# A decoder layer's tail in four pieces woven into the samples' attention, and branch A's scores for four chunks at once

## The chip, the cores and the metric

The kernel runs on one core of one Trainium2 chip. The metric is the device time of one execution in microseconds, the median of several. All data is float32.

## The reference, cut to what matters

One layer serves 1024 prompt tokens and 8 samples of 4 tokens each. The samples attend over 8192 cached tokens, in 64 pages of 128 per sample.

```python
u = rmsnorm(h); qa, kv_a, qi, ki, wi, qb, kv_b, g_a, g_b = project(u @ w_in)
# branch A: top-k keys by an indexer, then softmax(q k) v over 8 heads, 2 key heads of 64
# branch B: (softmax(Q1 K1) - lam softmax(Q2 K2)) V over 4 heads of 128, rmsnorm per head
merged = sigmoid(g_a) * (o_a @ w_br_a) + sigmoid(g_b) * (o_b @ w_br_b)
h = h + rmsnorm(merged @ w_out, attn_post_g)
gate, up = split(rmsnorm(h, ffn_pre_g) @ w_gate_up)
h = h + rmsnorm((silu(gate) * up) @ w_down, ffn_post_g)
y = h + sigmoid(h @ w_ple_gate) * (p_i @ w_ple_proj)
```

The lines from `merged` on are what this document calls the tail. They need only the attention's output `o` of the same token.

## The kernel before

Five engines run their own queues: TensorE (PE) multiplies, VectorE (DVE) and ScalarE (ACT) do the elementwise work, GpSimd (POOL) and SyncE (SP) mostly issue DMAs. They wait for each other by semaphores. The program is a sequence of stages, each a block whose end all engines meet: the projections, the prompt's selection and attention, the samples' attention (`sample_attend`), and the last stage (`tail`).

**The tail of the layer** is the class `Tail`. Tokens lie along columns, features along partitions. It works through pieces of columns; per piece there are units in a fixed order: `ma` and `mb` (the two branches' projections, 8 of each, alternating), `wo` (8), the norm `n1`, the updates `a1`, `n2`, `a2`, `gg` and `up` (22 of each), `d0`, `d1`, `dn` (the down projection, 8 outputs in three parts), `n3`, `a3`, then 8 times `yg`, `yp` and the transposition `yt` with the store of y. A unit has a number `g`; `at` finds it, `done_by` says which count of the semaphore `done` it raises. Every unit of weights is one DMA from `packed` into one of four slots (`SLOTS`): 256 KB for `ma` and `mb`, 512 KB for `wo`, `gg`, `up`, `yg`. SP issues the load for the unit four further on when a unit is done (`sync`, L1379). At the last `dn` of a piece SP issues the loads of o and of the gates for the next piece (`load_inputs`, L1383, L1387), and at its last `yt` those of h and of the embedding (`load_stream`, L1391, L1392). Two PSUM banks take turns. A float32 matmul shows as two records on PE.

**Who computes which columns.** `sample_attend` holds a `Tail` named `tw` with three pieces of 304 columns, prompt tokens 0 to 911. The last stage has its own `Tail` named `tp` with one piece of 144 columns: prompt tokens 912 to 1023 and the 32 samples' tokens.

**The samples' attention** goes through 64 chunks of 8 pages, 8 chunks per sample, in the steps that the list `steps` holds. A step has the scores of the chunk before, the transposition of this chunk's keys on DVE (`keys` in two parts for branch B, L1976, and `keys_a`, L1984), and the values of a chunk ten steps back. The scores of branch B (L1798) are 64 matmuls of 32x32 weights on 256 columns on all 16 places of the PE array: row group k by head h. The scores of branch A (L1808) wait for every second chunk: for `d` in 4 and `k` in 4 and the two chunks `i`, 32 matmuls on the 8 places k by i. After the fourth chunk of a half, ACT copies branch B's scores from the PSUM bank (`b_out`, L1917), DVE adds the selection to branch A's (`a_out`, L1993), reads both for the maxima (L1997), and at a sample's end the softmax follows.

**The order** is written out by a small planner: each unit of `tw` has a cost (`cost`), and each step gets an equal share of the sum of the costs less `LEAD` (20) and `RESERVE` (60); units are put between slots of a step as their budget allows, and the rest follow after the last step. All engines go through this one order; DVE and ACT take the units a little later (`late`). At the end SP stores the samples' attention output, `out_b` and `out_a`, to `o_t` in memory (L1777, L1779), and the last stage reads it back as columns of its o. The stretch between these two blocks is called the seam below.

Of the kernel before, what the change touches and what calls it, by code (L numbers as in the profile page):

```python
# [1296 lines left out]
STARTS = [0, WOVEN, 2 * WOVEN]  # L1297


class Tail:  # L1300
# [6 lines left out]
    def __init__(self, nc, a, ctx, name, ident, ones, banks, starts, width):  # L1307
        ph = Phase(nc, ctx, name)
        self.width, self.rows, self.left, self.nb, pieces = width, width // P, width % P, len(banks), starts
# [12 lines left out]
        for g, (p, kind, n) in enumerate(self.units):  # L1322
# [3 lines left out]
            if kind[0] != "a":  # L1326
# [8 lines left out]
        self.gates = self.x[:, KC:3 * KC].rearrange("p (g n) t -> p g n t", g=2)  # L1335
        self.w = ph.sb("w", [P, self.SLOTS, 8, P])
        self.ple = ph.sb("ple", [P, 2, width])
        self.y_t = ph.sb("y_t", [P, 2, width])
        self.y_row = ph.sb("y_row", [P, 2, self.rows + 1, P])
# [9 lines left out]
         self.rooted, self.normed, self.h_set, self.sig_set, self.y_set) = (  # L1349
            ph.sem(n) for n in ("done", "o_in", "gates_in", "h_in", "ple_in", "gains_in", "z_set", "squared", "summed", "changed",  # L1350
                                "rooted", "normed", "h_set", "sig_set", "y_set"))
# [14 lines left out]
    def cost(self, g):  # L1366
        p, kind, n = self.units[g]
        scale = self.width / 352
# [12 lines left out]
    def load_inputs(self, sp, p):  # L1381
        cols = slice(self.pieces[p], self.pieces[p] + self.width)
        sp.dma_start(self.o, self.a["o_t"].rearrange("(k p) t -> p k t", p=P)[:, :, cols]).then_inc(self.o_in, 16)  # L1383
        if p == 0:
            for at in range(self.SLOTS):
                self.load_weights(sp, at)
        sp.dma_start(self.gates, self.a["gate_t"][:, :, :, cols]).then_inc(self.gates_in, 16)  # L1387

    def load_stream(self, sp, p):
        cols = slice(self.pieces[p], self.pieces[p] + self.width)  # L1390
        sp.dma_start(self.h[:], self.a["xp_t"][:, 0:KC, cols]).then_inc(self.h_in, 16)  # L1391
        sp.dma_start(self.ple[:], self.a["xp_t"][:, KC:KC + 2, cols]).then_inc(self.ple_in, 16)  # L1392
# [8 lines left out]
    def sync(self, sp, g):  # L1401
# [7 lines left out]
        if kind == "yt":  # L1409
            sp.wait_ge(self.freed_by(g), self.freed_at(g))  # L1410
            first, full, end = self.pieces[p], self.pieces[p] + self.rows * P, self.pieces[p] + self.width
            cols = slice(n * P, (n + 1) * P)
            sp.dma_start(self.a["y"][first:full, cols].rearrange("(j p) c -> p j c", p=P), self.y_row[:, n % 2, 0:self.rows, :]).then_inc(self.stored[n % 2], 16)
            sp.dma_start(self.a["y"][full:end, cols], self.y_row[0:self.left, n % 2, self.rows, :]).then_inc(self.stored[n % 2], 16)
            if n == KC - 1 and p + 1 < len(self.pieces):
                self.load_stream(sp, p + 1)
# [5 lines left out]
    def tensor(self, pe, g):  # L1422
# [3 lines left out]
        bank = self.bank(g)  # L1426
        if self.freed_at(g) > 1:
            pe.wait_ge(self.freed_by(g), self.freed_at(g) - 1)
        if kind in ("n1", "n2", "n3"):
            pe.wait_ge(self.summed, 24 * p + {"n1": KC, "n2": 2 * KC, "n3": 3 * KC}[kind])  # L1430
            pe.matmul(bank[:, 0:self.width], self.ones[:], self.sumsq[:], start=True, stop=True).then_inc(self.done, 1)  # L1431
            return
        if kind == "yt":
            pe.wait_ge(self.y_set, p * KC + n + 1)
            for j in range(self.rows + 1):
                rows = min(P, self.width - j * P)
# [13 lines left out]
        for k in range(lo, hi):  # L1450
# [7 lines left out]
            ins = pe.matmul(bank[:, 0:self.width], self.w[:, at % self.SLOTS, k - lo, :], moving[:, k, :], start=(k == 0), stop=(k == depth - 1))  # L1458
        ins.then_inc(self.done, 1)

    def scalar(self, act, g):
        nc, (p, kind, n) = self.nc, self.units[g]
        bank = self.bank(g) if g in self.bank_of else None
        if kind in ("wo", "dn"):
# [4 lines left out]
            nc.scalar.activation(self.sq[:, i % 2], bank[:, 0:self.width], ACT.Square).then_inc(self.squared, 1)  # L1469
            nc.scalar.copy((self.u if kind == "wo" else self.z)[:, n], bank[:, 0:self.width]).then_inc(self.freed_by(g), 1)  # L1470
        if kind in ("n1", "n2", "n3"):
            act.wait_ge(self.freed_by(g), self.freed_at(g))
            nc.scalar.activation(self.rstd[:], self.rstd[:], ACT.Sqrt).then_inc(self.rooted, 1)  # L1473
        if kind == "a1":
# [3 lines left out]
            nc.scalar.activation(self.sq[:, i % 2], self.h[:, n], ACT.Square).then_inc(self.squared, 1)  # L1478
        if kind == "gg":
# [4 lines left out]
            nc.scalar.activation(self.sig[:, n % 2], bank[:, 0:self.width], ACT.Sigmoid).then_inc(self.sig_set, 1)  # L1484
        if kind == "yg":
# [3 lines left out]
            nc.scalar.activation(self.sig[:, n % 2], bank[:, 0:self.width], ACT.Sigmoid).then_inc(self.freed_by(g), 1)  # L1489
        if kind == "yt":  # L1490
# [3 lines left out]
            nc.scalar.copy(self.y_row[:, n % 2, 0:self.rows, :], bank[:, 0:self.rows * P].rearrange("p (j c) -> p j c", c=P))  # L1494
            nc.scalar.copy(self.y_row[0:self.left, n % 2, self.rows, :], bank[0:self.left, self.rows * P:(self.rows + 1) * P]).then_inc(self.freed_by(g), 1)

    def add_square(self, dve, i):
        nc = self.nc
        dve.wait_ge(self.squared, i + 1)
        dve.drain()  # L1500
        if i % KC == 0:
            nc.vector.tensor_copy(self.sumsq[:], self.sq[:, i % 2]).then_inc(self.summed, 1)
        else:
            nc.vector.tensor_tensor(self.sumsq[:], self.sumsq[:], self.sq[:, i % 2], ALU.add).then_inc(self.summed, 1)  # L1504

    def vector(self, dve, g):
        nc, (p, kind, n) = self.nc, self.units[g]
        bank = self.bank(g)[:, 0:self.width] if g in self.bank_of else None
        if kind == "ma":
            if n == 0:  # L1510
                dve.wait_ge(self.gates_in, 16 * (p + 1))
            dve.wait_ge(self.done, self.done_by[g])
            nc.vector.tensor_tensor(self.z[:, n], bank, self.gates[:, 0, n], ALU.mult).then_inc(self.freed_by(g), 1)
        if kind == "mb":
            dve.wait_ge(self.done, self.done_by[g])
            nc.vector.tensor_tensor(self.sig[:, n % 2], bank, self.gates[:, 1, n], ALU.mult).then_inc(self.freed_by(g), 1)
            dve.drain()
            nc.vector.tensor_tensor(self.z[:, n], self.z[:, n], self.sig[:, n % 2], ALU.add).then_inc(self.z_set, 1)
        if kind in ("wo", "dn"):
            self.add_square(dve, self.of_square(p, kind, n))  # L1520
        if kind in ("n1", "n2", "n3"):
# [6 lines left out]
            nc.vector.tensor_scalar(self.rstd[:], bank, 1.0 / D, 1e-6, ALU.mult, ALU.add).then_inc(self.freed_by(g), 1)  # L1528
            dve.wait_ge(self.rooted, 3 * p + which + 1)
            nc.vector.reciprocal(self.rstd[:], self.rstd[:])  # L1530
            dve.drain()
        if kind in ("a1", "a2", "a3"):
            gain = self.gains[:, int(kind[1]) - 1, n:n + 1]
            if kind == "a2":
                nc.vector.scalar_tensor_tensor(out=self.z[:, n], in0=self.h[:, n], scalar=gain, in1=self.rstd[:], op0=ALU.mult, op1=ALU.mult).then_inc(self.normed, 1)  # L1535
                return
            src = (self.u if kind == "a1" else self.z)[:, n]
            dve.drain()
            nc.vector.scalar_tensor_tensor(out=self.sig[:, n % 2], in0=src, scalar=gain, in1=self.rstd[:], op0=ALU.mult, op1=ALU.mult)  # L1539
            dve.drain()  # L1540
            nc.vector.tensor_tensor(self.h[:, n], self.h[:, n], self.sig[:, n % 2], ALU.add).then_inc(self.changed if kind == "a1" else self.h_set, 1)  # L1541
# [4 lines left out]
        if kind == "gg":  # L1546
            dve.wait_ge(self.sig_set, p * self.F_TILES + n + 1)
            nc.vector.tensor_tensor(self.sig[:, n % 2], bank, self.sig[:, n % 2], ALU.mult).then_inc(self.freed_by(g), 1)  # L1548
        if kind == "up":
            dve.wait_ge(self.done, self.done_by[g])  # L1550
            dve.drain()
            nc.vector.tensor_tensor(self.act_t[:, n], bank, self.sig[:, n % 2], ALU.mult).then_inc(self.freed_by(g), 1)
        if kind == "yp":
# [3 lines left out]
            nc.vector.tensor_tensor(self.sig[:, n % 2], bank, self.sig[:, n % 2], ALU.mult).then_inc(self.freed_by(g), 1)  # L1557
# [3 lines left out]
            nc.vector.tensor_tensor(self.y_t[:, n % 2], self.h[:, n], self.sig[:, n % 2], ALU.add).then_inc(self.y_set, 1)  # L1561
# [20 lines left out]
def sample_attend(nc, a):  # L1582
# [8 lines left out]
    with ExitStack() as ctx:  # L1591
# [10 lines left out]
        key_a = ph.sb("key_a", [P, 2 * CH, 4, 32])  # L1602
# [47 lines left out]
        rest = Tail(nc, a, ctx, "tw", ident, ones, t_bank, STARTS, WOVEN)  # L1650
# [12 lines left out]
        squared, ms_ready, meaned, rooted, finished, stored = (ph.sem(n) for n in ("squared", "ms", "meaned", "rooted", "finished", "stored"))  # L1663
# [31 lines left out]
        costs = [rest.cost(u) for u in range(len(rest.units))]  # L1695
# [13 lines left out]
        order += [("rest", u) for u in range(g, len(costs))]  # L1709
# [30 lines left out]
        def _(sp):  # L1740
# [44 lines left out]
        def _(pe):  # L1785
            def scores(c):
# [183 lines left out]
        def _(dve):  # L1970
# [8 lines left out]
            def turn_keys_a(c):  # L1979
                dve.wait_ge(ka_in[c % 2], (c // 2 + 1) * CH * 16)  # L1980
                if c % 2 == 0 and c:
                    dve.wait_ge(a_scored, c // 2)
                at = c % 2 * CH
                nc.vector.transpose(key_a[:, at:at + CH].rearrange("p g n s -> p (g n s)"),  # L1984
# [14 lines left out]
            def set_q(b):  # L1999
                if b:  # L2000
                    dve.wait_ge(a_scored, 4 * b)
# [219 lines left out]
```

## Time and profile before

| | us |
|---|---|
| median of 3 runs | 3236.38 (3230.28 to 3241.0) |
| profiled execution, its own time | 3238.8 |
| span of its trace | 3237.3 |
| PE busy | 2876.3 (89%) |
| DVE busy | 1461.4 (45%) |
| POOL, ACT busy | 678.3, 588.2 |
| records on PE | 26593 |

Busy is the time in which an engine had an instruction in work; matmuls overlap each other in the pipeline, so their mean duration is longer than the distance of their starts. The granted clock (PEclk) is given in tenths of the full TensorE clock over 40 equal slices of 80.9 us. In the views, `tw_` names are buffers of the woven tail, `tp_` those of the last stage, `sa_` those of the samples' attention; L numbers are lines of the kernel before.

### The profile page before, as it was taken

What the parts mean: (1) busy time and instruction counts of PE and PEld (TensorE: products, weight loads), DVE (VectorE), ACT (ScalarE), POOL (GpSimd) and SP (SyncE); (2) the same over time, 40 slices, a digit from 0 to 9 for tenths busy, and PEclk for the clock granted to TensorE, in tenths of its full rate; (3) what the DMA queues carried; (4) which work ended last, traced back from release to release, by engine and by line L of the source; (5) the groups of instructions that cost most, each with busy time, mean ns of one, the idle gap of its engine ahead of it and who ended that gap; (6) DMA issues with size and microseconds to landing.
All of it is one profiled execution on the core that took longest, in us unless ns stands there. A gap on an engine that the chain in (4) does not pass through costs nothing. (4 is left out here: it accounts for less than half of the span.)

```text
span 3237.3 us, 69341 instructions
## 1 busy us (share of the span) xinstructions
PE 2876.3 (89%) x26593; PEld 2020.4 (62%) x26593; DVE 1461.4 (45%) x3004; ACT 588.2 (18%) x1308; POOL 678.3 (21%) x1192
## 2 busy tenths in 40 slices
PE   8998979998789669999978889999798799998698
PEld 4764534665466446666755567766566576675698
DVE  2337858996788354333343443323433632002211
ACT  2431112001566110101011110010100201001101
POOL 0131003001100001133332433333333333430000
PEclk9999989999899889999998999999899899999799
DMA  7575239422500757789888988888888896662586
GB/s 226 148 226 181 79 117 305 128 79 87 164 8 18 223 182 245 241 299 315 297 303 271 310 297 276 308 305 302 300 282 276 268 300 235 223 204 91 174 266 197
DMA packets 419892, 708.73 MB, mean 219 GB/s; under 512 B 67985, under 2 KB 230193, under 8 KB 419442
## 3 DMA queue, kind: packets, MB, share of 16 engines
q1 hardware_dynamic: 330674, 470.65, 44.5%
q0 software_dynamic: 75456, 232.86, 21.7%
q8 instruction: 211, 3.46, 0.4%
q10 hardware_dynamic: 13440, 0.85, 0.3%
q14 instruction: 111, 0.91, 0.1%
HBM read 660.01 MB, written 92.13 MB: 232 GB/s over the span
## 5 line engine op out<-in xcount | busy, mean ns | idle before, releaser
L1458 PE MATMUL sa_t<-tw_z,tw_w 128*128 128x304 f32 x2496 | 679.8, 428 | 14.8 <-DVE tw_z L1535 10.7
L1458 PEld LDWEIGHTS sa_t<-tw_z,tw_w 128*128 128x128 f32 x2496 | 470.5, 192 | 195.3 <-issue 44.4
L1736 POOL DMA_DIRECT2D sa_ring_v<-cache_b_kv x512 | 275.2, 537 | 1211.5 <-PE sa_o L1865 850.4
L1458 PE MATMUL sa_t<-tw_x,tw_w 128*128 128x304 f32 x1440 | 406.0, 438 | 43.4 <-DMA tw_w<-packed 37.8
L1976 DVE STREAM_TRANSPOSE sa_key_b<-sa_ring_k 128x2048 f32<-128x2048 f32 x128 | 294.9, 2307 | 263.9 <-PE sa_s L1798 194.1
L1458 PEld LDWEIGHTS sa_t<-tw_x,tw_w 128*128 128x128 f32 x1440 | 277.5, 197 | 151.5 <-issue 64.6
L414 PE MATMUL pr_acc<-pr_w,pr_u_t 128*128 128x512 f32 (+1 forms) x720 | 288.1, 548 | 3.8 <-DVE pr_row L574 3.7
L1737 POOL DMA_DIRECT2D sa_ring_va<-cache_a_kv x512 | 274.2, 536 | 54.1 <-issue 27.0
L874 PE MATMUL sel_g<-sel_u,sel_gw 128*128 128x352 f32 x768 | 227.5, 459 | 0.0
L1798 PE MATMUL sa_s<-sa_key_b,sa_q_pad 32*32 32x256 f32 x8192 | 191.9, 416 | 26.1 <-DVE sa_key_b L1976 19.3
L874 PEld LDWEIGHTS sel_g<-sel_u,sel_gw 128*128 128x128 f32 x768 | 145.8, 190 | 81.9 <-issue 0.8
L414 PEld LDWEIGHTS pr_acc<-pr_w,pr_u_t 128*128 128x128 f32 x720 | 125.3, 198 | 112.8 <-issue 108.3
L1798 PEld LDWEIGHTS sa_s<-sa_key_b,sa_q_pad 32*32 32x32 f32 x8192 | 123.7, 107 | 82.1 <-issue 32.1
L1861 PE MATMUL sa_o<-sa_ring_v,sa_prob_t 128*8 128x128 f32 x4096 | 142.5, 280 | 26.3 <-DMA sa_ring_va<-cache_a_kv 19.9
L1861 PEld LDWEIGHTS sa_o<-sa_ring_v,sa_prob_t 128*8 128x8 f32 x4096 | 102.1, 91 | 78.3 <-issue 54.6
L1484 ACT ACTIVATE tw_sig<-sa_t 128x304 f32<-128x304 f32 x66 | 28.0, 424 | 542.7 <-PE sa_t L1458 542.7
L1458 PE MATMUL sa_t<-tw_h,tw_w 128*128 128x304 f32 x384 | 113.3, 450 | 12.8 <-DVE tw_h L1541 5.6
L1548 DVE TENSOR_TENSOR tw_sig<-sa_t,tw_sig 128x304 f32<-128x304 f32 x66 | 30.9, 468 | 190.3 <-ACT tw_sig L1484 190.0
L1458 PE MATMUL ta_bank<-tp_z,tp_w 128*128 128x144 f32 x832 | 105.3, 291 | 3.6 <-DVE tp_z L1535 2.4
L1458 PEld LDWEIGHTS ta_bank<-tp_z,tp_w 128*128 128x128 f32 x832 | 104.8, 194 | 4.3 <-issue 4.3
L1504 DVE TENSOR_TENSOR tw_sumsq<-tw_sumsq,tw_sq 128x304 f32<-128x304 f32 x63 | 30.0, 476 | 171.2 <-ACT tw_sq L1469 166.2
L1469 ACT ACTIVATE tw_sq<-sa_t 128x304 f32<-128x304 f32 x48 | 20.3, 423 | 463.3 <-PE sa_t L1458 463.3
(336 smaller groups left out, 3499.7 us busy)
## 6 DMA issues: line engine op xcount, KB each, us to landing
sa_ring_k<-cache_b_kv SPq DMA_DIRECT2D x512, 256.0 KB, 4.0
sa_ring_v<-cache_b_kv POOLq DMA_DIRECT2D x512, 256.0 KB, 6.3
tw_w<-packed SPq DMA_DIRECT2D x228, 512.0 KB, 6.5
tp_w<-packed SPq DMA_DIRECT2D x76, 512.0 KB, 4.3
sa_ring_ka<-cache_a_kv SPq DMA_DIRECT2D x512, 64.0 KB
sa_ring_va<-cache_a_kv POOLq DMA_DIRECT2D x512, 64.0 KB, 6.2
packed<-w_gate_up POOLq DMA_DIRECT2D x44, 512.0 KB, 13.7
tw_w<-packed SPq DMA_DIRECT2D x48, 256.0 KB, 7.5
```

What stands on the lines that cost most here:

```text
L414: ins = pe.matmul(acc[m % ACC][:, 0:hi - lo], u_t[:, p % 2, k, :], w[:, k, lo:hi], start=(k == 0), stop=(k == KC - 1))
L874: ins = pe.matmul(g_bank[n % 4][:, 0:PIECE], gw[j % GATE_W][:, k, :], u[:, k, c * PIECE:(c + 1) * PIECE], start=(k == 0), stop=(k == KC - 1))
L1458: ins = pe.matmul(bank[:, 0:self.width], self.w[:, at % self.SLOTS, k - lo, :], moving[:, k, :], start=(k == 0), stop=(k == depth - 1))
L1469: nc.scalar.activation(self.sq[:, i % 2], bank[:, 0:self.width], ACT.Square).then_inc(self.squared, 1)
L1484: nc.scalar.activation(self.sig[:, n % 2], bank[:, 0:self.width], ACT.Sigmoid).then_inc(self.sig_set, 1)
L1504: nc.vector.tensor_tensor(self.sumsq[:], self.sumsq[:], self.sq[:, i % 2], ALU.add).then_inc(self.summed, 1)
L1548: nc.vector.tensor_tensor(self.sig[:, n % 2], bank, self.sig[:, n % 2], ALU.mult).then_inc(self.freed_by(g), 1)
L1736: pool.dma_start(ring_v[:, n % RING, :], rows_of(cache_b, page, 1)).then_inc(v_in[n // 4 % 2], 16)
L1737: pool.dma_start(ring_va[:, n % RING, :], rows_of(cache_a, page, 1)).then_inc(va_in[n // 4 % 2], 16)
L1798: ins = pe.matmul(s_bank[32 * h:32 * h + 32, k, 0:CH * 32], q_pad[rows, d, h, 24 - 8 * j:56 - 8 * j], key_b[rows, :, 4 * h + d, :], start= ...
L1861: pe.matmul(o_bank[32 * h:32 * h + 8, 0:P], prob_t[:, g, 0, at:at + 8], ring_v[:, g, h * P:(h + 1) * P], start=False, stop=False, tile_pos ...
L1976: nc.vector.transpose(key_b[:, at:at + 4].rearrange("p g n s -> p (g n s)"), ring_k[:, at:at + 4, :].rearrange("p g e -> p (g e)")).then_i ...
```

## The change

The `Tail` takes pieces as pairs of columns, each with its own width, and `sample_attend` gets a fourth, 912 to 1056. The stage `tail` is empty. The planner's costs count three pieces as before; the fourth follows after everything. The samples' part of o isn't stored and read back: a new slot `join`, after the last `a3` of the third piece, copies `out_b` and `out_a` into the columns of o on DVE. The load of the gates is two DMAs, one for each gate. `key_a` holds four chunks, and branch A's scores are computed at each fourth chunk, on 16 places.

```diff
-STARTS = [0, WOVEN, 2 * WOVEN]
+PIECES = [(0, WOVEN), (WOVEN, 2 * WOVEN), (2 * WOVEN, 3 * WOVEN), (3 * WOVEN, TOK)]
...
     def load_inputs(self, sp, p):
-        cols = slice(self.pieces[p], self.pieces[p] + self.width)
-        sp.dma_start(self.o, self.a["o_t"].rearrange("(k p) t -> p k t", p=P)[:, :, cols]).then_inc(self.o_in, 16)
+        cols, w = slice(*self.pieces[p]), self.widths[p]
+        prompt = slice(cols.start, min(cols.stop, SEQ))
+        sp.dma_start(self.o[:, :, 0:prompt.stop - prompt.start], self.a["o_t"].rearrange("(k p) t -> p k t", p=P)[:, :, prompt]).then_inc(self.o_in, 16)
         if p == 0:
             for at in range(self.SLOTS):
                 self.load_weights(sp, at)
-        sp.dma_start(self.gates, self.a["gate_t"][:, :, :, cols]).then_inc(self.gates_in, 16)
+        for g in range(2):
+            sp.dma_start(self.gates[:, g, :, 0:w], self.a["gate_t"][:, g, :, cols]).then_inc(self.gates_in, 16)
...
         if kind == "ma" and n == 0:
             pe.wait_ge(self.o_in, 16 * (p + 1))
+            if self.pieces[p][1] > SEQ:
+                pe.wait_ge(self.joined, 1)
...
+    def join_samples(self, dve, out_a, out_b):
+        nc, cols = self.nc, slice(self.sample_lo, self.sample_lo + NB * NQ)
+        last = len(self.pieces) - 2
+        dve.wait_ge(self.done, self.done_by[self.at[last, "dn", KC - 1]])
+        dve.drain()
+        nc.vector.tensor_copy(self.o[:, 4:8, cols], out_b[:])
+        for g in range(HKV):
+            for half in range(2):
+                src = out_a[g * DH:(g + 1) * DH].rearrange("p (g r e) t -> p g r e t", g=HKV, e=2)[:, g, :, half]
+                ins = nc.vector.tensor_copy(self.o[half * DH:(half + 1) * DH, 2 * g:2 * g + 2, cols], src)
+        ins.then_inc(self.joined, 1)
...
-        key_a = ph.sb("key_a", [P, 2 * CH, 4, 32])
+        key_a = ph.sb("key_a", [P, 4 * CH, 4, 32])
...
-        costs = [rest.cost(u) for u in range(len(rest.units))]
+        alone = rest.at[len(PIECES) - 1, "ma", 0]
+        costs = [rest.cost(u) for u in range(alone)]
...
-        order += [("rest", u) for u in range(g, len(costs))]
+        for u in range(g, len(rest.units)):
+            order += [("rest", u)]
+            if u == rest.at[len(PIECES) - 2, "a3", KC - 1]:
+                order += [("join",)]
...
-            sp.wait_ge(finished, 1)
-            sp.dma_start(a["o_t"][512:1024, SEQ:TOK].rearrange("(h e) t -> e h t", e=P), out_b[:]).then_inc(stored, 16)
-            for g in range(HKV):
-                sp.dma_start(a["o_t"][g * 256:(g + 1) * 256, SEQ:TOK].rearrange("(r d) t -> d r t", d=DH),
-                             out_a[g * DH:(g + 1) * DH, g * 4:(g + 1) * 4, :]).then_inc(stored, 16)
-            sp.wait_ge(stored, 48)
             rest.sync_end(sp)
...
                 ins.then_inc(scored, 1)
-                if j % 2 == 0:
+                if j < 3:
                     return
                 pe.wait_ge(turned_a, c + 1)
                 for d in range(4):
                     for k in range(4):
                         rows = slice(32 * k, 32 * k + 32)
-                        for i in (j - 1, j):
-                            ins = pe.matmul(s_bank[32 * i:32 * i + 32, k, CH * 32:2 * CH * 32], q_a[rows, d, :], key_a[rows, i % 2 * CH:(i % 2 + 1) * CH, d, :],
+                        for i in range(4):
+                            ins = pe.matmul(s_bank[32 * i:32 * i + 32, k, CH * 32:2 * CH * 32], q_a[rows, d, :], key_a[rows, i * CH:(i + 1) * CH, d, :],
                                             start=False, stop=(d == 3), tile_position=(32 * k, 32 * i), skip_group_check=True)
...
-                act.wait_ge(a_scored, 2 * n + 2)
+                act.wait_ge(a_scored, n + 1)
...
-                if c % 2 == 0 and c:
-                    dve.wait_ge(a_scored, c // 2)
+                if c % 4 == 0 and c:
+                    dve.wait_ge(a_scored, c // 4)
```

The other edits give every slice of a buffer its piece's width, and `tail` becomes `del nc, a`.

## Rows read from the trace of the kernel before

**Rows 1.** The page: span, busy share and count, granted clock in 40 slices.
```profile
span 3237.3 us, 69341 instructions
...
PE 2876.3 (89%) x26593; PEld 2020.4 (62%) x26593; DVE 1461.4 (45%) x3004; ACT 588.2 (18%) x1308; POOL 678.3 (21%) x1192
...
PEclk9999989999899889999998999999899899999799
```

**Rows 2.** Windows, samples' stage: start:end, length, busy by engine, clock, DMA share, GB/s.
```profile
1150.00:2705.00 1555.00, 1390.56 (x18419) 991.42 (x18418) 617.89 (x756) 190.44 (x370) 472.14 (x880) 0.95 0.85 285
2705.00:2990.30 285.30, 265.20 (x1759) 190.62 (x1758) 40.99 (x90) 32.65 (x71) 77.24 (x144) 0.97 0.54 177
```

**Rows 3.** PE's waits from 1150 to 2705: us in total, times, longest.
```profile
PE sa_t L1458 <- DMA tw_w<-packed: 24.8, 10, 7.4
PE sa_t L1431 <- DVE tw_sumsq L1504: 22.3, 6, 7.4
PE sa_s L1798 <- DVE sa_key_b L1976: 19.3, 3, 11.3
...
PE sa_o L1861 <- DMA sa_ring_va<-cache_a_kv: 12.4, 4, 5.0
```

**Rows 4.** Timeline of the seam: start, duration, engine, line, count, idle time before.
```profile
2989.75 0.52 PE L1437 MATMUL sa_t<-sa_ident,tw_y_t 128*128 128x128 f32 x3 [0.97 <-DVE tw_y_t L1561]
...
2996.55 0.37 SPq L1383 DMA_DIRECT2D tp_x<-o_t  x1
...
3002.09 4.18 PE L1458 MATMUL ta_bank<-tp_x,tp_w 128*128 128x144 f32 x16 [11.82 <-DMA tp_w<-packed]
...
3008.73 0.31 DVE L1513 TENSOR_TENSOR tp_z<-ta_bank,tp_x 128x144 f32<-128x144 f32 x1 [11.91 <-DMA tp_x<-gate_t]
3009.09 8.12 PE L1458 MATMUL ta_bank<-tp_x,tp_w 128*128 128x144 f32 x48 [2.83 <-DVE tp_z L1513]
...
3020.51 11.45 PE L1458 MATMUL ta_bank<-tp_x,tp_w 128*128 128x144 f32 x64 [3.30 <-DMA tp_w<-packed]
...
3033.13 15.92 PE L1458 MATMUL ta_bank<-tp_z,tp_w 128*128 128x144 f32 x128 [1.17 <-DMA tp_w<-packed]
```

**Rows 5.** Windows of the last stage.
```profile
3002.00:3033.00 31.00, 23.69 (x128) 22.54 (x128) 7.30 (x24) 0.00 (x0) 0.00 (x0) 0.77 0.71 210
3033.00:3050.00 17.00, 16.00 (x129) 15.84 (x129) 2.40 (x8) 4.12 (x17) 0.00 (x0) 1.00 0.88 276
3088.00:3198.00 110.00, 109.91 (x897) 109.81 (x896) 12.86 (x42) 8.15 (x31) 0.00 (x0) 1.00 0.84 265
```

**Rows 6.** DMA issues of the last stage: count, size, median us to landing.
```profile
tp_w<-packed SPq DMA_DIRECT2D x16, 256.0 KB, 4.6
```

**Rows 7.** Timeline around the third piece's last update, and a small DVE copy.
```profile
2091.59 0.17 DVE L2008 COPY sa_q_a<-sa_q_raw_a 128x32 f32<-128x32 f32 x1
...
2944.89 0.47 DVE L1541 TENSOR_TENSOR tw_h<-tw_h,tw_sig 128x304 f32<-128x304 f32 x1
...
2947.32 0.47 DVE L1557 TENSOR_TENSOR tw_sig<-sa_t,tw_sig 128x304 f32<-128x304 f32 x1 [1.96 <-PE sa_t L1458]
```

**Rows 8.** Groups of score matmuls: count, busy us, mean ns, idle before.
```profile
L1798 PE MATMUL sa_s<-sa_key_b,sa_q_pad 32*32 32x256 f32 x8192 | 191.9, 416 | 26.1 <-DVE sa_key_b L1976 19.3 <-issue 6.8
L1808 PE MATMUL sa_s<-sa_key_a,sa_q_a 32*32 32x256 f32 x2048 | 81.2, 383 | 11.4 <-issue 11.2
```

**Rows 9.** Timeline of PE: branch B's scores alone, then with branch A's behind.
```profile
1456.59 2.76 PE L1798 MATMUL sa_s<-sa_key_b,sa_q_pad 32*32 32x256 f32 x128
1459.28 8.45 PE L1458 MATMUL sa_t<-tw_z,tw_w 128*128 128x304 f32 x32
...
1478.66 2.56 PE L1798 MATMUL sa_s<-sa_key_b,sa_q_pad 32*32 32x256 f32 x116
...
1483.14 0.24 PE L1815 MATMUL sa_stat<-sa_k_new,sa_q_new 128*32 128x4 f32 x8
```

**Rows 10.** Timeline of DVE at the end of a half.
```profile
1995.02 1.23 DVE L1993 TENSOR_TENSOR sa_raw<-sa_s,sa_sel 128x1024 f32<-128x1024 f32 x1 [0.45 <-ACT sa_raw L1917]
```

More of the change, by code:

```diff
@@ L1305, with __init__ @@
     F_TILES = D_FF // P
-    def __init__(self, nc, a, ctx, name, ident, ones, banks, starts, width):
+    def __init__(self, nc, a, ctx, name, ident, ones, banks, pieces):
         ph = Phase(nc, ctx, name)
-        self.width, self.rows, self.left, self.nb, pieces = width, width // P, width % P, len(banks), starts
+        width, self.nb = max(hi - lo for lo, hi in pieces), len(banks)
+        self.widths = [hi - lo for lo, hi in pieces]
         self.nc, self.a, self.ident, self.ones, self.banks, self.pieces = nc, a, ident, ones, banks, pieces
@@ L1367, in cost @@
         p, kind, n = self.units[g]
-        scale = self.width / 352
+        scale = self.widths[p] / 352
         if kind in self.KINDS:
@@ L1410, in sync @@
             sp.wait_ge(self.freed_by(g), self.freed_at(g))
[L1411 to L1414, printed above, removed]
+            first, end = self.pieces[p]
+            rows, left = self.widths[p] // P, self.widths[p] % P
+            full, cols = first + rows * P, slice(n * P, (n + 1) * P)
+            sp.dma_start(self.a["y"][first:full, cols].rearrange("(j p) c -> p j c", p=P), self.y_row[:, n % 2, 0:rows, :]).then_inc(self.stored[n % 2], 16)
+            sp.dma_start(self.a["y"][full:end, cols], self.y_row[0:left, n % 2, rows, :]).then_inc(self.stored[n % 2], 16)
             if n == KC - 1 and p + 1 < len(self.pieces):
@@ L1425, in tensor @@
             return
-        bank = self.bank(g)
+        bank, w = self.bank(g), self.widths[p]
         if self.freed_at(g) > 1:
@@ L1430, in tensor @@
             pe.wait_ge(self.summed, 24 * p + {"n1": KC, "n2": 2 * KC, "n3": 3 * KC}[kind])
-            pe.matmul(bank[:, 0:self.width], self.ones[:], self.sumsq[:], start=True, stop=True).then_inc(self.done, 1)
+            pe.matmul(bank[:, 0:w], self.ones[:], self.sumsq[:, 0:w], start=True, stop=True).then_inc(self.done, 1)
             return
@@ L1434, in tensor @@
             pe.wait_ge(self.y_set, p * KC + n + 1)
-            for j in range(self.rows + 1):
-                rows = min(P, self.width - j * P)
+            for j in range(w // P + 1):
+                rows = min(P, w - j * P)
                 ins = pe.transpose(bank[0:rows, j * P:(j + 1) * P], self.y_t[:, n % 2, j * P:j * P + rows], self.ident[:])
@@ L1462, in scalar @@
         nc, (p, kind, n) = self.nc, self.units[g]
-        bank = self.bank(g) if g in self.bank_of else None
+        bank, w = self.bank(g) if g in self.bank_of else None, self.widths[p]
         if kind in ("wo", "dn"):
@@ L1493, in scalar @@
                 act.wait_ge(self.stored[n % 2], 32 * (p * KC // 2 + n // 2))
-            nc.scalar.copy(self.y_row[:, n % 2, 0:self.rows, :], bank[:, 0:self.rows * P].rearrange("p (j c) -> p j c", c=P))
-            nc.scalar.copy(self.y_row[0:self.left, n % 2, self.rows, :], bank[0:self.left, self.rows * P:(self.rows + 1) * P]).then_inc(self.freed_by(g), 1)
+            rows, left = w // P, w % P
+            nc.scalar.copy(self.y_row[:, n % 2, 0:rows, :], bank[:, 0:rows * P].rearrange("p (j c) -> p j c", c=P))
+            nc.scalar.copy(self.y_row[0:left, n % 2, rows, :], bank[0:left, rows * P:(rows + 1) * P]).then_inc(self.freed_by(g), 1)
     def add_square(self, dve, i):
-        nc = self.nc
+        nc, w = self.nc, self.widths[i // 24]
         dve.wait_ge(self.squared, i + 1)
@@ L2117, in _ @@
                     dve.drain()
-                    nc.vector.scalar_tensor_tensor(out=flat, in0=flat, scalar=gain[:, 0:1], in1=rms[:, 0], op0=ALU.mult, op1=ALU.mult).then_inc(finished, 1)
+                    nc.vector.scalar_tensor_tensor(out=flat, in0=flat, scalar=gain[:, 0:1], in1=rms[:, 0], op0=ALU.mult, op1=ALU.mult)
+                elif slot[0] == "join":
+                    rest.join_samples(dve, out_a, out_b)
 def tail(nc, a):
-    with ExitStack() as ctx:
-        ph = Phase(nc, ctx, "ta")
-        ones = ph.sb("ones", [P, P])
-        ident = ph.sb("ident", [P, P])
-        banks = [ph.ps(f"bank{c}", [P, 512]) for c in range(2)]
-        id_clear, ident_ready, ones_ready = ph.sem("id_clear"), ph.sem("ident"), ph.sem("ones")
-        rest = Tail(nc, a, ctx, "tp", ident, ones, banks, [len(STARTS) * WOVEN], TOK - len(STARTS) * WOVEN)
-        block = ctx.enter_context(nc.Block())
-        @block.gpsimd
-        def _(pool):
-            identity_on(nc, pool, ident, id_clear, ident_ready)
-        @block.sync
-        def _(sp):
-            rest.sync_begin(sp)
-            for g in range(len(rest.units)):
-                if g == 4:
-                    rest.load_stream(sp, 0)
-                rest.sync(sp, g)
-            rest.sync_end(sp)
-        @block.tensor
-        def _(pe):
-            pe.wait_ge(ident_ready, 1)
-            pe.wait_ge(ones_ready, 1)
-            for g in range(len(rest.units)):
-                rest.tensor(pe, g)
-        @block.scalar
-        def _(act):
-            rest.scalar_begin(act)
-            for g in range(len(rest.units)):
-                rest.scalar(act, g)
-        @block.vector
-        def _(dve):
-            nc.vector.memset(ones[:], 1.0).then_inc(ones_ready, 1)
-            for g in range(len(rest.units)):
-                rest.vector(dve, g)
+    del nc, a
 _WEIGHTS = ("w_in", "w_br_a", "w_br_b", "w_out", "w_gate_up", "w_down", "w_ple_gate", "w_ple_proj",
```

70 lines of the change are left out of this document (36 added, 34 removed).

## Prediction

> **What bounds the kernel now.** I read the page first: the span, the busy shares and the granted clock [rows 1]. TensorE (PE) is busy 89% of the span, and no other engine comes near. Then the windows by stage [rows 2]. From 1150 to 2705 us, where the samples' scores are made while three prompt pieces of the layer's tail are woven in, PE is busy 1390.6 of 1555 us and the DMA engines carry 285 GB/s at a share of 0.85. So PE sets the pace there, with DMA close behind. From 2705 to 2990 PE is busy 265 of 285 us. The waits of PE in the first stretch [rows 3] say what most of the other 164 us are: weights of the tail 24.8 us, the norms' sums 22.3, transposed keys 19.3, values of branch A 12.4, smaller ones below. No single wait carries the stretch; a saving of PE time there is worth most of itself, except next to a wait on DMA.
>
> The second thing the reader should see is the seam before the last stage [rows 4]. The last PE work of the samples' block ends at 2989.75 + 0.52 = 2990.3. The first load of the last stage is issued at 2996.55, PE starts at 3002.09 (11.82 us idle, on weights), idles 2.83 us more because VectorE (DVE) waits for the gates until 3008.73, then 3.30 us on weights. The `wo` units begin at 3033.13. So 42.8 us pass for the 16 `ma`/`mb` units, 128 PE records. The windows show what they cost without the seam [rows 5]: 31 us at a granted clock of 0.77 for those 128 records, against 897 records in 109.9 us at clock 1.00 later in the same stage, 0.1227 us each. The 128 would be 15.7 us of PE.
>
> **Part 1, the last stage as fourth piece.** Its units, widths (144 columns) and weight loads are those of the stage before; `wo` and all that follows cost what they did, and I leave them alone. What changes lies between 2990.3 and the first `wo`. Gone are the three stores of the samples' rows and the wait for them, the end of one block and the start of another, the first loads with nothing before them. The four weight slots are full at the seam, because the loads for `ma` 0 to `mb` 1 go out as the last `yg`/`yp` units of piece 3 finish. The loads of o's prompt rows and of the gates go out at piece 3's last `dn` unit, ahead of its third norm and all its `yg` and `yp` units. `ma` 0 can start at 2990.3.
>
> Then the loads must keep up. A unit of `ma` or `mb` is 8 records, 0.98 us. Its 256 KB load is issued when the unit four before it is done and lands 4.6 us later (median, [rows 6]). Four units therefore take 0.98 + 4.6 + about 0.1 for the issue = 5.7 us instead of 3.9. The first four wait for nothing, so the last four start at 3 x 5.7 = 17.1 and all are done at 21.0 us. Now SP's queue: it has the last y stores of piece 3, then h and the embedding (8 and 2 blocks of 128 x 144 x 4 bytes, 576 and 144 KB, two issues of about 0.5 us each) ahead of `ma` 2's weights, and their bytes share the engines: 720 KB at 210 to 276 GB/s [rows 5] is about 3 us. 24 us in all. The saving is 42.8 - 24 = 19 us. Its upper end is no wait at all: 42.8 - 15.7 = 27. Its lower end is that these units take as long as before, 3002.09 to 3033.13 = 31.0 us: 11.8, say 12. I take 19, by the landing row, which is the nearest.
>
> **The join.** Five small DVE copies replace the stores and the read back. DVE's copies of 32 columns took 0.17 us [rows 7]; the one of 128 columns lies between that and the 0.47 us of an operation on 304. Together about 1 us. They stand after the last `a3` update (2944.89 + 0.47) and before the `yp` product at 2947.32, ahead of which DVE idled 1.96 us [rows 7]. So they cost nothing; were that cover gone, the `yp` product, PE's second bank and so `yg` 1 would be late by 1 us once. Its wait on the last `dn` is met before the norm that stands ahead of it. Range 0 to 1 us. The gates as two loads instead of one per piece add one issue of SP of about 0.5 us, three times ahead of loads that PE isn't waiting for at that moment: 0 to 2 us, taken as 0. The woven order before the join doesn't move, since the budget still counts three pieces.
>
> **Part 2, scores of branch A for four chunks at once.** The same 2048 PE records remain [rows 8]; only how many run beside each other changes, 8 places of the array before, 16 after. The timeline prices it [rows 9]: scores of branch B alone, 128 records on 16 places, take 1456.59 to 1459.28 = 2.69 us. The same with a pair of chunks of branch A behind it takes 1478.66 to 1483.14 = 4.48 us. A pair, 64 records on 8 places, so costs 1.79 us. Four chunks now are 128 records on 16 places with the same shape as branch B's row, so 2.69. Per four chunks 2 x 1.79 - 2.69 = 0.89 us, times 16 = 14.2 us of PE.
>
> What of it reaches the end? Of PE's waits in that stretch 37 us are on DMA [rows 3], at places where a faster PE only waits longer, and the DMA share is already 0.85. I take three quarters, 11 us. Added is a wait: ScalarE's copy of the scores now waits for the four-chunk group, which ends 0.89 us later than the pair did. Behind it are DVE's addition of the selection (which idled 0.45 us for it at 1995.02, [rows 10]), the maxima, and behind those the transposed keys for the next chunk. PE reads these one step later, about 1555/64 = 24 us, so it is covered; without cover it costs up to 0.89 us at each of the 8 ends of a sample, 7 us. The end range is 14 down to -7.
>
> Here a rule speaks for a larger number. The Trainium skill, "TensorEngine Tiling (Array Packing)", section Theoretical Speedup, lets 32x32 tiles run independently, up to 16 times. By it four chunks would cost what two do, 1.79 us, and the part would bring 28.6 us. The trace disagrees for branch B's 16 places: 2.69 us for 8 records per place, 1.5 times the pair's 1.79 for also 8 records per place.
>
> **Sum.** 19 + 11 = 30 us. Against the profiled execution (3238.8, of which the span is 3237.3 and 1.5 lie around it): 3208.8. The median of the runs is 2.4 us lower, so 3206.
>
> **Rivals.**
> - The fourth piece starts at 2990.3, but waits on weights lower the clock as they did from 3002 to 3033 (0.77), and its first 16 units take 31 us. For it: with 5.7 us per four units PE is busy only 69% there. Against it: that clock followed 12 us of a PE at rest, and now there is none. 12 + 11 = 23: 3213. Chance 0.20.
> - The scores' gain is lost since DMA paces the stretch. For it: the share of 0.85 with windows of waits on weights and values. Against it: all PE waits on DMA are 2.4% of the stretch. 19 + 0: 3217. Chance 0.12.
> - The fourth piece never waits for weights, and all of the PE time counts: 27 + 14 = 41: 3195. For it: later in the stage the same four slots keep PE at full rate [rows 5]. Against it: a unit of 256 KB is only 0.98 us of PE. Chance 0.13.
> - Sixteen places cost no more than eight (1.79 us per group): 19 + 28.6 = 48: 3189. Against it is branch B's row. Chance 0.07.
> - Slower: the four-chunk group holds ScalarE's copy, DVE stops at its addition with the next key transposition queued behind, and PE stops at the next scores. Place: `b_out`, `a_out`, `turn_keys`, at 16 half ends. Before, PE waited for these keys 3 times, 19.3 us, the longest 11.3 [rows 3], so the two others 4.0 each. If all 16 cost 4.0 it loses 64 us against 30: 3270; it decides from 30/16 = 1.9 us each. Against it: the copy is only 0.89 us late, and a step is 24 us. Chance 0.02.
> - Both parts at their lower ends (12 - 7 = 5): 3231, no change that can be told. Chance 0.03.
>
> **How the numbers follow.** The forecast keeps 0.43, with its own range of 3200 to 3212. Within 0.3% (10 us) a measurement of this kernel can't tell a change. All cases but the last two lie over that: faster 0.95, same 0.03, slower 0.02. The range takes in the cases of 12 + 0 (3224) above, and below most of the way to the sixteen places' case: 3192 to 3224.
>
> **What would show it.** PE's rows at the seam: no idle over 2 us between the last transpose of piece 3 and `ma` 0; first `ma` to first `wo` in 20 to 28 us, with waits on `tw_w` about 5 us in sum. A four-chunk group of branch A: 128 records in about 2.7 us. DVE idle before the first `yp` product falls from 1.96 to about 1. Wrong: a first `wo` later than 31 us after the seam, groups of 3.5 us or more, or new waits of PE on key transposes. The stretch to the last scores shorter by less than 5 us would refute the three quarters.

## The result and the profile after

The change makes the kernel slightly slower: 3250.95 us (median of 7, 3242.29 to 3257.73) against 3236.38 (7, 3216.41 to 3241.48). The ratio is 1.0047, 95% interval 1.0027 to 1.0067. Forecast were 3206 us and a gain of 30. The profiled execution took 3257.73 us.

The page of the changed kernel, the lines that answer to [rows 1], and the count of instruction packets, which was 211 before as well:

```profile
span 3256.1 us, 69289 instructions
...
PE 2874.4 (88%) x26593; PEld 2011.4 (62%) x26593; DVE 1462.0 (45%) x3008; ACT 588.1 (18%) x1308; POOL 677.6 (21%) x1190
...
PEclk9999989998899889999999899999889899999899
...
q8 instruction: 211, 3.46, 0.4%
```

PE has the same 26593 records and is busy 2 us less; the span is 18.8 us longer. So PE idles more. The windows say where, beside [rows 2] and [rows 5]; the first ends with the last scores, the third is from the seam to the first `wo`, the fourth is `wo`:

```profile
1150.00:2739.40 1589.40, 1395.15 (x18414) 985.04 (x18414) 617.65 (x755) 190.31 (x370) 472.03 (x880) 0.93 0.83 279
2739.40:3024.60 285.20, 264.60 (x1764) 190.79 (x1763) 41.88 (x95) 32.79 (x72) 77.24 (x144) 0.98 0.57 186
3024.60:3049.50 24.90, 18.56 (x129) 17.42 (x128) 7.39 (x24) 0.53 (x2) 0.00 (x0) 0.93 0.69 216
3049.50:3067.00 17.50, 17.47 (x128) 17.40 (x128) 2.09 (x7) 3.22 (x14) 0.00 (x0) 0.90 0.75 248
```

The stretch with the scores grew from 1555.0 to 1589.4 us, the one behind it stayed at 285, and seam to `wo` shrank from 42.8 to 24.9. So the first part came as forecast (18 us for 19) and the second cost 34 us where 11 of gain were put.

The seam in the timeline of PE, answering to [rows 4]:

```profile
3024.10 0.52 PE L1442 MATMUL sa_t<-sa_ident,tw_y_t 128*128 128x128 f32 x3 [0.97 <-DVE tw_y_t L1570]
3024.45 4.09 PE L1465 MATMUL sa_t<-tw_x,tw_w 128*128 128x144 f32 x32
3031.53 9.34 PE L1465 MATMUL sa_t<-tw_x,tw_w 128*128 128x144 f32 x56 [2.98 <-DMA tw_w<-packed]
3042.47 4.16 PE L1465 MATMUL sa_t<-tw_x,tw_w 128*128 128x144 f32 x32 [1.61 <-DMA tw_w<-packed]
3046.83 1.22 PE L1465 MATMUL sa_t<-tw_x,tw_w 128*128 128x144 f32 x8 [0.20 <-DMA tw_w<-packed]
3049.53 17.59 PE L1465 MATMUL sa_t<-tw_z,tw_w 128*128 128x144 f32 x128 [1.48 <-DMA tw_w<-packed]
```

`ma` 0 starts without a pause, and the first four units run on full slots (32 records in 4.09 us). The first load behind them is 2.98 us late; the forecast had 1.8 us there for the landing and 3 for SP's queue. In sum PE waits 6.3 us (2.98 + 1.61 + 0.20 + 1.48) where the forecast had 8.3, and is busy 18.6 us where it had 15.7, at a granted clock of 0.93.

The join, on DVE, beside [rows 7]:

```profile
2979.80 0.23 DVE L1577 COPY tw_x<-sa_out_b 128x128 f32<-128x128 f32 x1
2979.94 0.79 DVE L1581 COPY tw_x<-sa_out_a 64x64 f32<-64x64 f32 x4
...
2981.67 0.47 DVE L1566 TENSOR_TENSOR tw_sig<-sa_t,tw_sig 128x304 f32<-128x304 f32 x1 [0.94 <-PE sa_t L1465]
```

One us in all, in a gap of DVE that shrank from 1.96 to 0.94. It cost nothing.

Now the waits of PE in the first stretch, beside [rows 3]:

```profile
PE sa_s L1827 <- issue: 34.2, 11, 3.8
PE sa_t L1465 <- DMA tw_w<-packed: 26.9, 9, 6.8
PE sa_o L1880 <- DMA sa_ring_va<-cache_a_kv: 22.3, 8, 5.3
PE sa_t L1436 <- DVE tw_sumsq L1512: 16.9, 6, 6.1
PE sa_s L1817 <- DVE sa_key_b L1995: 16.6, 3, 8.4
```

A new row leads. L1827 is branch A's group, and "issue" means that nothing which the profile shows as a releaser was missing. In the kernel before the same row stood in sixth place, in the same stretch:

```profile
PE sa_s L1808 <- issue: 11.2, 6, 3.3
```

[rows 8] show these 11.2 us too, as part of 11.4 us of idle time; the prediction doesn't ask what they are.

One group in the timeline of PE (the lines left out hold one or two records each where the groups overlap, and the last 12 of branch B):

```profile
2090.23 4.36 PE L1465 MATMUL sa_t<-tw_z,tw_w 128*128 128x304 f32 x16
2094.52 2.54 PE L1817 MATMUL sa_s<-sa_key_b,sa_q_pad 32*32 32x256 f32 x115
...
2096.92 1.45 PE L1827 MATMUL sa_s<-sa_key_a,sa_q_a 32*32 32x256 f32 x41
2101.76 3.35 PE L1827 MATMUL sa_s<-sa_key_a,sa_q_a 32*32 32x256 f32 x84 [3.39 <-issue]
```

PE stops in the middle of the group, after 44 of its 128 records. No semaphore stands there: the group's only wait is ahead of its first matmul. What happens on the DMA side, in the window from 2099 to 2100 us:

```profile
q1 hardware_dynamic: 53, 0.21, 54.3%
q0 software_dynamic: 51, 0.16, 41.5%
q8 instruction: 1, 0.02, 6.8%
```

A packet of instructions is under way, with the data queues full around it. q8 carries PE's instructions, as the counts say: its queue shows 54183 entries in the trace (matmul records, weight loads and what the sequencer does), and 211 packets make that 257 to a packet of 16 KB. Two groups of 128 records back to back are 512 entries with their weight loads and want two packets within 5.4 us; a unit of the tail, 16 records in 4.3 us, wants one in 34.

The places of the stalls bear this out. Count PE's entries in order of their start. When PE goes on after each of the 12 stalls at L1827, the entries already started are 193 or 194 more than a multiple of 256, and the number of packets started by then is that same multiple: at 1285.42 us it is 50 x 256 + 193 entries and 50 packets. The last of these packets started 2.2 to 2.8 us before PE went on and itself took about 1 us. So PE stops at the end of a packet's instructions and goes on after the next packet has come. The same holds, without an exception, for all 79 breaks of over 0.3 us inside a run of score matmuls in the traces of ten kernels (before, changed, e1 to e8). What makes the next packet start so late is not shown.

### The profile page after: what moved, and what is told of

Read it like the earlier page. It is cut to its first block, busy times and chain, and to the rows that moved or that the text cites. A ratio compares the mean times of both kernels' runs of the same rounds, so it can differ in the third digit from the quotient of the medians.

```text
span 3256.1 us, 69289 instructions
## 1 busy us (share of the span) xinstructions
PE 2874.4 (88%) x26593; PEld 2011.4 (62%) x26593; DVE 1462.0 (45%) x3008; ACT 588.1 (18%) x1308; POOL 677.6 (21%) x1190
## 3 DMA queue, kind: packets, MB, share of 16 engines
q8 instruction: 211, 3.46, 0.4%
## 4 chain that ended last, share of the span: by engine, by line
PE 48%; DMA 5%; DVE 4%; issue 4%; SPq 3%; ACT 1%; DVEq 1%; POOLq 0%; POOL 0%; ACTq 0%
PE sa_t L1465 36%; PE sa_s L1817 4%; PE sa_o L1880 3%; DMA tw_w<-packed 3%; PE sa_s L1827 2%; DMA sa_ring_k<-cache_b_kv 1%; DMA sa_ring_va<-cache_a_kv 1%; SPq L1773 1%; PE sa_stat L1857 1%; SPq L1774 1%; DVE tw_sig L1548 1%; DVE sa_key_b L1995 1%; PE sa_o L1884 1%; ACT sa_prob_t L1956 1%; DVE tw_h L1550 1%
## 5 line engine op out<-in xcount | busy, mean ns | idle before, releaser
L1465 PE MATMUL sa_t<-tw_z,tw_w 128*128 128x304 f32 (+1 forms) x3328 | 787.7, 395 | 24.0 <-DVE tw_z L1544 13.6
L1465 PEld LDWEIGHTS sa_t<-tw_z,tw_w 128*128 128x128 f32 x3328 | 577.7, 194 | 206.2 <-issue 51.9
L1465 PE MATMUL sa_t<-tw_x,tw_w 128*128 128x304 f32 (+1 forms) x1920 | 471.5, 404 | 49.7 <-DMA tw_w<-packed 44.6
L1465 PEld LDWEIGHTS sa_t<-tw_x,tw_w 128*128 128x128 f32 x1920 | 341.6, 198 | 160.1 <-issue 75.1
L1465 PE MATMUL sa_t<-tw_h,tw_w 128*128 128x304 f32 (+1 forms) x512 | 136.9, 419 | 19.1 <-DVE tw_h L1550 10.4
L1491 ACT ACTIVATE tw_sig<-sa_t 128x304 f32<-128x304 f32 (+1 forms) x88 | 34.4, 390 | 618.4 <-PE sa_t L1465 618.4
L1512 DVE TENSOR_TENSOR tw_sumsq<-tw_sumsq,tw_sq 128x304 f32<-128x304 f32 (+1 forms) x84 | 36.4, 433 | 228.0 <-ACT tw_sq L1476 222.4
L1557 DVE TENSOR_TENSOR tw_sig<-sa_t,tw_sig 128x304 f32<-128x304 f32 (+1 forms) x88 | 37.6, 428 | 223.8 <-ACT tw_sig L1491 223.6
L1465 PEld LDWEIGHTS sa_t<-tw_h,tw_w 128*128 128x128 f32 x512 | 93.8, 206 | 58.2 <-issue 19.5
L1561 DVE TENSOR_TENSOR tw_x<-sa_t,tw_sig 128x304 f32<-128x304 f32 (+1 forms) x88 | 38.1, 433 | 168.8 <-PE sa_t L1465 166.1
## 6 DMA issues: line engine op xcount, KB each, us to landing
packed<-w_gate_up POOLq DMA_DIRECT2D x44, 512.0 KB, 14.2
```

The source lines that it names most:

```text
L1465: ins = pe.matmul(bank[:, 0:w], self.w[:, at % self.SLOTS, k - lo, :], moving[:, k, 0:w], start=(k == 0), stop=(k == depth - 1))
L1512: nc.vector.tensor_tensor(self.sumsq[:, 0:w], self.sumsq[:, 0:w], self.sq[:, i % 2, 0:w], ALU.add).then_inc(self.summed, 1)
L1557: nc.vector.tensor_tensor(sig[:, n % 2], bank, sig[:, n % 2], ALU.mult).then_inc(self.freed_by(g), 1)
L1561: nc.vector.tensor_tensor(self.act_t[:, n, 0:w], bank, sig[:, n % 2], ALU.mult).then_inc(self.freed_by(g), 1)
```

## The experiments

Each kernel was timed beside the kernel before; all ratios are to it. The medians of the kernel before in the three sets of experiments were 3232.5 (e1 to e4), 3233.0 (e5 to e7) and 3232.4 (e8 and e3 again). The last column is read from the whole trace; the rows of waits above end before the last of the changed kernel's stalls and have 34.2 of its 36.4 us. e5 and e6 leave out work of the layer.

| kernel | median us | ratio (95%) | idle "issue" at branch A's scores, us |
|---|---|---|---|
| changed | 3250.95 | 1.0047 (1.0027 to 1.0067) | 36.4 |
| e1 seam only | 3216.57 | 0.9949 (0.9930 to 0.9967) | 11.3 |
| e2 four chunks only | 3265.25 | 1.0108 (1.0074 to 1.0143) | 34.9 |
| e3 group apart | 3200.29 | 0.9904 (0.9871 to 0.9937) | 0.4 |
| e4 group in halves | 3249.60 | 1.0051 (1.0032 to 1.0071) | 0 |
| e5 fewer bytes | 3178.47 | 0.9836 (0.9809 to 0.9863) | 24.6 |
| e6 half as much ahead | 3190.92 | 0.9866 (0.9839 to 0.9893) | 11.9 |
| e7 pairs apart | 3217.26 | 0.9959 (0.9944 to 0.9974) | 2.8 |
| e8 maxima later | 3205.13 | 0.9926 (0.9901 to 0.9952) | 0.4 |
| e3 again | 3198.62 | 0.9897 (0.9877 to 0.9918) | 0.4 |

**e1, seam only.** Branch A in pairs again:

```diff
-                if j < 3:
+                if j % 2 == 0:
...
-                        for i in range(4):
-                            ins = pe.matmul(..., key_a[rows, i * CH:(i + 1) * CH, d, :],
+                        for i in (j - 1, j):
+                            ins = pe.matmul(..., key_a[rows, i % 2 * CH:(i % 2 + 1) * CH, d, :],
```

> The changed kernel with branch A's scores in pairs of chunks again (8 places, key_a of two chunks); the merged fourth piece and the join stay. Theory S (the seam gave its 18 us, and the four-chunk scores took them back and more): about 3218 us, ratio to the kernel before 0.9945; piece 3 ends near 2990 us as before, first ma to first wo about 25 us; PE's idle 'issue' time before branch A's scores back to about 11 us from 36. Rival M (the merged order itself delays the samples' stretch): the end of piece 3 stays near 3020 us and the ratio at 1.00 or above.

3216.57 us, 0.9949: the seam alone gives 16 us. The last transpose of piece 3 ends at 2973.0 and the first `wo` starts at 2997.27, 24.2 us later. Theory S holds, rival M falls.

**e2, four chunks only.** The same lines the other way, in the kernel before.

> The kernel before with only branch A's scores for four chunks at once; the last stage stays a stage of its own. Theory S: the scores alone cost what the samples' stretch grew by, 34 us in the profile, so about 3236 + 25 to 35 = 3266 us, ratio 1.008 to 1.011, with some 34 us of PE idle on 'issue' before branch A's scores. Rival M: ratio at 0.996 to 1.000, as the forecast of this part had it.

3265.25 us, 1.0108. The two parts add up: -0.0051 + 0.0108 = +0.0057, within the interval of the whole. So the four-chunk scores cost some 33 to 35 us on their own, and the stalls are there without the merged piece: 34.9 us.

**e3, group apart.** The order gets a slot of its own for branch A's group, with at least 4 us of tail units ahead:

```diff
+            step += [("scores_a", s - 1)] if 0 < s <= CHUNKS and s % 4 == 0 else []
...
+                between = 0.0
+                while slot[0] == "scores_a" and between < 4.0 and g < len(costs):
+                    order.append(("rest", g))
+                    spent += costs[g]
+                    between += costs[g]
+                    g += 1
                 order.append(slot)
```

> The changed kernel, but branch A's four-chunk group no longer stands right behind branch B's scores: at least one unit of the tail (4 us of PE, few instructions) is put between. Theory I (PE runs out of instructions: 512 of them in 5.4 us, and the next 16 KB block of instructions lands too late): the idle 'issue' time before branch A's scores falls from 36 to under 10 us, the group takes 2.7 to 2.8 us, and the time falls by 25 to 35 us to 3215 to 3225, ratio 0.991 to 0.997. Rival P (sixteen places at once collide in PSUM or on their operands, or the copy behind them is late): the stall within the group stays at 3 us each and the ratio at 1.00 or more.

3200.29 us, better than the expected 3215 to 3225, and 3198.62 when run again: 16 to 18 us under e1 and about 1% under the kernel before. Its stretch up to the last scores is 53 us shorter than the changed kernel's. 33 of them are idle time of PE (161.3 for 194.2 us), and 20 are busy time, at a granted clock of 0.95 for 0.93. The same place in its timeline:

```profile
2072.30 2.76 PE L1824 MATMUL sa_s<-sa_key_b,sa_q_pad 32*32 32x256 f32 x128
2074.99 4.36 PE L1465 MATMUL sa_t<-tw_z,tw_w 128*128 128x304 f32 x16
2079.28 2.76 PE L1834 MATMUL sa_s<-sa_key_a,sa_q_a 32*32 32x256 f32 x128
2081.97 0.25 PE L1841 MATMUL sa_stat<-sa_k_new,sa_q_new 128*32 128x4 f32 x8
```

The group takes 2079.28 to 2081.97 = 2.69 us, to the hundredth what branch B's row had promised, and is not interrupted. The work in it is the same; only what stands ahead of it has changed. Rival P, a collision of sixteen places, falls. Stalls on "issue" are left elsewhere, 6.7 us before the values (L1887) among them.

**e4, group in halves.** As e3, with `d` 0 and 1 in one slot and `d` 2 and 3 in a second, tail units between.

> As the kernel with the group apart, but the group itself is cut in two halves (d 0 and 1, d 2 and 3) with another unit of the tail between. Theory I: no stalls on 'issue' in either half, the same as the kernel with the group apart or up to 10 us faster. Rival P: each half of 64 records stalls or is slower than 1.35 us; ratio at 1.00 or more.

3249.60 us, a miss: no stall in branch A's halves (7.5 us are left before branch B's scores, in 3 places), and yet 50 us slower than e3. Its waits in the same stretch:

```profile
PE sa_stat L1848 <- DVE sa_top L2055: 39.8, 7, 9.2
PE sa_t L1465 <- DMA tw_w<-packed: 29.1, 6, 11.9
PE sa_s L1824 <- DVE sa_key_b L2005: 28.0, 7, 11.2
```

This is akin to the slower rival of the prediction, in another kernel: the scores end two tail units after branch B's, and at a sample's end PE waits for DVE's maxima, 39.8 us in this window, where it was 0.5 in the changed kernel. The rival's own link, the transposed keys, has 28.0 us for 16.5 in e3. One tail unit of lateness already cost something (in e3 the wait on the maxima is 14.3 us), two cost more than they gave. The waits aren't all of the 50 us: the stretch is 58 us longer than e3's, 34 of them idle and 25 busy, at a granted clock of 0.93 for 0.95.

**e5, fewer bytes.** `pool.dma_start(ring_v[:, n % RING, 0:P], rows_of(cache_b, page, 1)[:, 0:P])`, the ring cleared once.

> The changed kernel, but of each page of branch B's values only a quarter is loaded (128 of 512 columns, the rest of the ring is set to zero once), 101 MB less in the samples' stretch. Leaves out three heads' values. Theory I with the load as cause (the block of instructions lands late because the DMA engines are full): the idle 'issue' time before branch A's scores falls below 15 us from 36. Theory I with the rate as cause (PE drinks 512 instructions faster than blocks can follow, loaded or not): it stays at 25 to 40 us. In both the time falls since values no longer wait: by 10 to 60 us.

The stalls stay at 24.6 us in 12 places, near the 25 of the rate's side and far from 15.

```profile
PE sa_s L1830 <- issue: 24.6, 12, 3.8
```

With 101 MB less they are a third shorter, so a fuller DMA lengthens them. It isn't shown to be their cause, since as many places stall as before. But the DMA share was still 0.72 here for 0.83 (1150 to 2700 us), so what an idle DMA would leave of them is open.

**e6, half as much ahead.** `for d in range(2 if j == 3 else 4)` in branch B's scores.

> The changed kernel, but branch B's scores just ahead of the four-chunk group do only half of their matmuls (d 0 and 1 of 4), in each fourth chunk. Leaves out half of that chunk's branch B scores. The two groups still stand back to back on 16 places, with 384 instructions in place of 512. Theory I: the idle 'issue' time before branch A's scores falls from 36 to what the pair had with 384 instructions, 8 to 16 us; beside the 16 x 1.35 = 22 us of PE left out the time falls by 25 us more, to about 3200. Rival P (two groups on 16 places back to back collide): 30 to 40 us of stall stay, and only the 22 us go.

```profile
PE sa_s L1827 <- issue: 11.9, 5, 4.0
```

11.9 us in 5 places, with one more stall of 3.5 us right behind a group, and 3190.92 us: 60 us for 22 us of matmuls left out. The stretch is 59 us shorter: 26 us of idle time (168.4 for 194.2), 24 of work left out, and 9 since less of the busy time lay at the lower clock. Both groups still stand back to back on the sixteen places; only their count fell, and with it the stalls. So it is the count of instructions back to back that decides, not the sixteen places.

**e7, pairs apart.** The slot of e3 for each pair of e1.

> The seam-only kernel (branch A in pairs of chunks on 8 places) with the same gap put between branch B's scores and each pair. Theory I: the 11 us of 'issue' before the pairs go too, a pair takes 1.75 us, and the time falls from 3217 by 10 to 25 us to 3192 to 3207. The kernel with the four-chunk group apart then gains only 14 us from its 16 places, or less, since it pays for 16 gaps and this for 32. Rival (the gap itself buys what it buys by the order around it, whatever the instructions): no change from 3217, within 5 us.

Here the rival holds. The pairs' stalls went from 11.3 to 2.8 us, but the time stayed (3217.26 against 3216.57). The wait for the maxima, 0.3 us in e1, took their place:

```profile
PE sa_stat L1848 <- DVE sa_top L2055: 14.7, 4, 6.0
...
PE sa_s L1835 <- issue: 2.8, 1, 2.8
```

e3 pays the same wait and is still 17 us faster, 20 by the ratio of its second run. So 16 places do bring a gain once instructions keep up, and my 14.2 us fit it. The sizes aren't separated further: the two ratios' intervals together allow 6 to 29 us (12 to 28 with the second run), and e7 has 32 gaps where e3 has 16.

**e8, maxima later.** In e3, `("top_rows", b)` stands behind the values' second part.

> The kernel with the four-chunk group apart, with one more move: at a sample's end the transposition of the maxima (top_rows) comes after the second part of the values instead of before it. There PE waited 14.3 us on DVE's maxima (4 times, longest 6.0), since the gap makes them later. Theory: PE works on values and tail units meanwhile, this wait falls below 4 us, and the time falls by 5 to 12 us to about 3188 to 3195, ratio 0.987 to 0.989. Rival: the wait only moves to the next link of the sample's end (the shifts or the exponentials behind it), and the time stays within 4 us of 3200.

3205.13 against 3198.62 for e3 beside it: not faster, and slower if anything (the two intervals overlap). Most of the wait moved a link on, as the rival said, though the time came out 5 us over the rival's 3200:

```profile
PE sa_stat L1853 <- DVE sa_top_rows L2063: 20.6, 6, 9.2
...
PE sa_stat L1847 <- DVE sa_top L2054: 8.0, 3, 4.2
```

> The same kernel as the one with the four-chunk group apart, run beside the one with the later maxima, for a comparison on one chip. Expected again at a ratio of 0.990 to the kernel before.

The version that beats both kernels is e3.

## Why the prediction was wrong

**What bounds the kernel: right.** PE paces the stretch, and a change of its time there reaches the end. Whether that is in full or three quarters, as I had counted, stays open: e3 against e7 gives 17 to 20 us, with intervals that hold 14.2, and 11 in the first run.

**The seam: right in mechanism, and in size with some luck.** 24.9 us for a forecast of 24, 17.9 saved for 19; e1 timed 16. Two errors within it cancelled: PE waited 2 us less for weights than forecast (6.3 for 8.3), and its work took 2.9 us more (18.6 for 15.7), 1.7 of them since the clock was 0.93 and not the 1.00 of the rows that I had priced it by. (The 0.1227 us per record comes out with 896 records, not 897; it changes nothing.) The `wo` units took 17.6 us for 15.9 at a granted clock of 0.90, which I had left alone; that is the small rest. The rival with 31 us at a clock of 0.77 did not come, but its direction did.

**The join, the gates, the order of units: right**, all at nothing as far as can be told: e1's 16 us leave no room for a cost that shows.

**The scores: the step that failed.** I priced four chunks at 2.69 us by branch B's row, and the price was right for a group that stands alone. What I left out is that in this kernel the group stands right behind branch B's, and that two such groups use up instructions faster than they arrive: 12 of the 16 groups were cut by a stall, 36.4 us in all, and e2 timed the part at 33 to 35 us lost where 11 were to be gained. The term was not mis-sized; a cost was missing from it, put at nothing without a reason. The account of the stretch, 34.4 us longer:

- PE's work, counted as if always at full clock, fell by 15.8 us (1316.8 for 1332.6), for a forecast of 14.2.
- Idle time of PE 194.2 for 164.4 us, +29.8. Of it "issue" at branch A's scores +23.0 (34.2 for 11.2) and the wait on branch A's values +9.9 (22.3 for 12.4); the rest comes to -3.1.
- The clock: the granted clock of the stretch fell from 0.95 to 0.93. The trace's record of the clock has PE busy for 157 us at the lower of its two levels (1.2 GHz), 116 before; 41 us more at half speed cost 20 us. That is why PE was busy for 1395.2 us, 4.6 more than before, with less work.

The sum is 29.8 + 20.4 - 15.8 = 34.4 us. So the kernel lost more than the stalls' own length. That the clock fell because of the stalls isn't shown, and the instruction stalls alone don't carry it: e4 has none in branch A's groups and 151 us of busy time at the lower level, e6 has about as many as the kernel before and 138 us. In these kernels it goes with the idle time of PE as a whole. The three kernels with 190 to 195 us idle in this stretch (changed, e2, e4) have 151 to 159 us at the lower level, those with 150 to 165 us idle have 96 to 118, and e6 with 168 lies between. No run held one of the two and moved the other.

The Trainium skill, "Runtime: NRT & Kernel Launch", section Instruction fetch mechanics, says that instructions come in 16 KiB blocks and that the cost of crossing a block's end is mostly hidden. The blocks agree (211 packets, 3.46 MB); "hidden" does not hold for groups of 21 ns per record, where a crossing showed as 2.2 to 3.9 us of idle PE in 11 of the 16 groups, and as 0.6 us in one.

**The added wait: half right.** ScalarE's copy came later, and it cost nothing noticeable in the changed kernel (0.5 us for the maxima both times). But the cover was thinner than the 24 us of a step that I gave: in e3 one tail unit of lateness (4 us) brought 14.3 us of waiting for the maxima, in e4 two brought 39.8.

**The slower rival** had the right sign and the wrong mechanism, at a chance of 0.02. The hint was in the profile: 11.2 us of "issue" in 6 stalls on L1808, up to 3.3 us each, exactly at groups of 128 and 64 records back to back. A change that puts 256 back to back had to be priced from that row: if each of the 16 groups lost 3.3 us, 53 us less 14, slower.

## What to carry to other kernels

Idle time on "issue" within a run of short PE instructions is a resource like any other; count the records per us that an edit puts back to back, and price it from the stalls already there. Packing small matmuls densely paid here only with something slow, a large matmul unit, between the dense groups. And a gap that cures one wait spends the slack of the chain behind it: one unit cost less than it gave, two cost more.

## What the hardware showed beyond that

A packet of PE's instructions is short (about 1 us), yet PE went on only 2.2 to 2.8 us after it had started, with 101 MB less to load as well as without (e5: 2.3 to 2.7 us). What differs between the stalls is how early the packet starts: in the changed kernel 10 of the 12 packets at its stalls started 0.4 to 1.3 us after PE had already stopped, in e5 only 2 of 12. With 384 instructions back to back 5 of 16 places stalled (e6; 6 of 32 in the kernel before), with 512 it was 12 of 16.
